# First block's merge: the sum of two gated branches by GpSimd, rounding and remainder of the merged tile one unit later

## The reference, cut to what matters

```python
merged = (jax.nn.sigmoid(g_a) * (y_a @ w_br_a)
          + jax.nn.sigmoid(g_b) * (y_b @ w_br_b)
          + jax.nn.sigmoid(g_c) * (y_c @ w_br_c))
return merged @ w_out
```

## Time and profile before

| what | value |
|---|---|
| median of 3 runs | 3005.26 us (3005.05 to 3005.29) |
| span of the profiled execution | 3003.9 us |
| median of the runs less that span | 1.36 us |
| TensorE busy | 2897.1 us, 96% |
| VectorE busy | 2051.9 us, 68% |
| ScalarE busy | 1366.5 us, 45% |
| GpSimd busy | 153.3 us, 5% |
| merge of layer 0, from its fourth unit to the first product of `out0` | 208.81 to 242.26 us |
| merge of layer 1, likewise | 670.78 to 704.27 us |

### The profile page before, as it was taken

How to read it: one execution, slowest core, us unless ns; L and a number is a source line. 1 busy time by engine, 2 the same in 40 slices (tenths; PEclk the granted TensorE clock), 3 DMA queues, 4 the chain that set the end, 5 groups by cost and what they waited for, 6 DMA issues and landing times.

```text
span 3003.9 us, 59994 instructions
## 1 busy us (share of the span) xinstructions
PE 2897.1 (96%) x23648; PEld 2789.5 (93%) x23648; DVE 2051.9 (68%) x3323; ACT 1366.5 (45%) x2212; POOL 153.3 (5%) x222
## 2 busy tenths in 40 slices
PE   8999999999999999999999999999999999899998
PEld 8889999888999999998889999999999999779998
DVE  4658786658678777778764476867768566876655
ACT  5555445555446432354544354223542235545543
POOL 0000000000000000010000020000200001000000
PEclk9999999999999999999999999999999999999999
DMA  6435764435666565552212354544645445225454
GB/s 235 146 115 187 243 235 163 149 108 176 211 210 198 193 222 194 177 184 67 81 45 89 105 185 161 206 156 171 208 162 207 144 152 187 64 82 192 161 184 138
DMA packets 148053, 487.54 MB, mean 162 GB/s; under 512 B 16400, under 2 KB 25872, under 8 KB 147728
## 3 DMA queue, kind: packets, MB, share of 16 engines
q1 hardware_dynamic: 126688, 407.22, 41.0%
q0 software_dynamic: 21168, 77.60, 7.6%
HBM read 482.66 MB, written 1.05 MB: 161 GB/s over the span
## 4 chain that ended last, share of the span: by engine, by line
PE 82%; DVE 9%; ACT 4%; issue 3%; DMA 2%; POOL 0%; DVEq 0%; ACTq 0%; SPq 0%; POOLq 0%
PE bank L2042 23%; PE bank L2043 22%; PE bank L2044 22%; DVE wlo L1141 3%; ACT whi L606 2%; PE bank L1960 2%; PE bank L1961 2%; PE bank L1962 2%; DVE acc L1742 2%; PE aux L2269 1%; PE bank L2287 1%; DMA bbb<-in_w_ada 1%; PE bank L2120 1%; DMA raw<-in_w_stream 1%; DMA big<-in_w_ada 1%
## 5 line engine op out<-in xcount | busy, mean ns | idle before, releaser
L2042 PE MATMUL bank<-uhi,whi 128*128 128x256 f32 x4968 | 1397.0, 281 | 9.6 <-DVE wlo L1141 6.0
L2044 PE MATMUL bank<-uhi,wlo 128*128 128x256 f32 x4968 | 1381.1, 278 | 0.0
L2043 PE MATMUL bank<-ulo,whi 128*128 128x256 f32 x4968 | 1380.9, 278 | 0.0
L1141 DVE TENSOR_TENSOR wlo<-raw,whi 128x1024 fp32r<-128x1024 f32 (+4 forms) x850 | 951.0, 1121 | 370.7 <-ACT whi L606 362.2
L2042 PEld LDWEIGHTS bank<-uhi,whi 128*128 128x128 f32 x4968 | 935.1, 188 | 28.2 <-issue 22.9
L606 ACT CAST whi<-raw 128x1024 fp32r<-128x1024 f32 (+4 forms) x850 | 811.5, 961 | 282.7 <-PE bank L2044 179.3
L2043 PEld LDWEIGHTS bank<-ulo,whi 128*128 128x128 f32 x4968 | 934.8, 188 | 3.4 <-issue 3.0
L2044 PEld LDWEIGHTS bank<-uhi,wlo 128*128 128x128 f32 x4968 | 937.7, 189 | 0.0
L2042 PE MATMUL bank<-yhi,whi 128*128 128x256 f32 x1740 | 494.1, 284 | 16.2 <-DVE wlo L1141 8.5
L2043 PE MATMUL bank<-ylo,whi 128*128 128x256 f32 x1764 | 491.3, 279 | 0.0
L2044 PE MATMUL bank<-yhi,wlo 128*128 128x256 f32 x1740 | 484.5, 278 | 0.0
(11 more groups left out here) (297 smaller groups left out, 2939.0 us busy)
## 6 DMA issues: line engine op xcount, KB each, us to landing
raw<-in_w_stream SPq DMA_DIRECT2D x674, 512.0 KB, 3.7
big<-in_w_ada POOLq DMA_DIRECT2D x64, 512.0 KB, 3.6
vt<-in_w_ada POOLq DMA_DIRECT2D x51, 512.0 KB, 3.7
raw<-in_w_stream SPq DMA_DIRECT2D x80, 256.0 KB, 2.7
raw<-in_w_stream SPq DMA_DIRECT2D x48, 384.0 KB, 3.1
bbb<-in_w_ada POOLq DMA_DIRECT2D x29, 512.0 KB, 4.7
raw<-in_w_stream SPq DMA_DIRECT2D x32, 192.0 KB, 2.4
raw<-in_w_stream SPq DMA_DIRECT2D x16, 128.0 KB, 2.0
```

The source lines that it names most:

```text
L1141: ve.tensor_tensor(wlo[:, u % SLOTS, 0:n], raw[:, u % SLOTS, 0:n], whi[:, u % SLOTS, 0:n].bitcast(F32), ALU.subtract).then_inc(s_low, 1)
L2042: te.matmul(out_, whi[:, u % SLOTS, w], hi(k)[:, cols], start=k == 0, stop=False)
L2043: te.matmul(out_, whi[:, u % SLOTS, w], lo(k)[:, cols], start=False, stop=False)
L2044: ins = te.matmul(out_, wlo[:, u % SLOTS, w], hi(k)[:, cols], start=False, stop=k == plan.kt[u] - 1)
```

## The change

GpSimd gets a part `merge_pairs(l)`, ahead of its wait for the merge's last unit: for each tile m it waits until the banks of units 3m and 3m + 1 are read (that is, until both gatings are done), adds the two gated branches in place, and gives `s_paired`. VectorE waits for it behind the third gating and makes only the second sum. The rounding of tile m moves on ScalarE from unit 3m + 2 to unit 3m + 3, behind the cast of that unit's `high`, and the remainder on VectorE to the same unit, behind its `low` and gating. For the last tile both stay at unit 23. The gated branches of tiles with even and odd m now lie in different rows of `lg` (0 to 3 and 4 to 7), the merged tile in the fourth of each.

```diff
+MERGE_ROWS = 4
...
+            def merge_pairs(l):
+
+                for m in range(DT):
+                    at = MERGE_ROWS * (m % 2)
+                    pool.wait_ge(*after(U[f"merge{l}"] + 3 * m))
+                    pool.wait_ge(*after(U[f"merge{l}"] + 3 * m + 1))
+                    nc.gpsimd.tensor_tensor(lg[:, at, :], lg[:, at, :], lg[:, at + 1, :], ALU.add).then_inc(s_paired, 1)
+
...
             for name, (first, per, _, _) in plan.ada.items():
+                if name in ("up00", "up10"):
+                    merge_pairs(int(name[2]))
...
-                def evac_m(j, i):
-                    if j % 3 == 2:
-                        val.wait(1)
-                        sc.copy(x1hi[:, 4 * i + j // 3, :], lg[:, 3 + (j // 3) % 2, :]).then_inc(s_ahi, 1)
-                    if j in (4, 7, 10) and isinstance(i, int) and i == 0:
+                def merged(m):
+                    val.wait(1)
+                    sc.copy(x1hi[:, m, :], lg[:, MERGE_ROWS * (m % 2) + 3, :]).then_inc(s_ahi, 1)
+
+                def evac_m(j):
+                    if j % 3 == 0 and j:
+                        merged(j // 3 - 1)
+                    if j in (4, 7, 10):
                         gate_rows(1, (j - 4) // 3)
+                    if j == 23:
+                        merged(DT - 1)
...
-                    ve.tensor_tensor(lg[:, br, :], gates[br][:, m, :], bank(u0, j)[:, 0:S],
+                    ve.tensor_tensor(lg[:, at + br, :], gates[br][:, m, :], bank(u0, j)[:, 0:S],
                                      ALU.mult).then_inc(read(u0, j), 1)
+                    if br == 0 and m:
+                        merged_rest(m - 1)
                     if br == 2:
-                        dve.wait_ge(*after_at(u0, j, i, 12))
-                        mg = lg[:, 3 + (j // 3) % 2, :]
-                        chained(ve.tensor_tensor(lg[:, 0, :], lg[:, 0, :], lg[:, 1, :], ALU.add))
-                        ve.tensor_tensor(mg, lg[:, 0, :], lg[:, 2, :], ALU.add).then_inc(s_val, 1)
+                        dve.wait_ge(*after(u0 + j))
+                        dve.wait_ge(s_paired, DT * l + m + 1)
+                        ve.tensor_tensor(lg[:, at + 3, :], lg[:, at, :], lg[:, at + 2, :], ALU.add).then_inc(s_val, 1)
                         if m == DT - 2:
                             low(u0 + 21 + AHEAD)
-                        ahi.wait(1)
-                        rest(x1lo[:, m, :], mg, x1hi[:, m, :])
+                        if m == DT - 1:
+                            merged_rest(m)
```

More of the change, by code:

```diff
@@ L446, in program @@
         s_hbias = sem("half_bias_ready")
+        s_paired = sem("merge_pair_added")
         ring1 = [bbb[:, 4 * r:4 * r + 4, :] for r in range(2)]
@@ L846, in _ @@
                         high(um + 21 + AHEAD)
-                    evac_m(j % 12, j // 12)
+                    evac_m(j)
                 norm1(f"out{l}", p1("ln1_g", l, DT), p1("ln1_b", l, DT))
@@ L1577, in _, with merged_rest, evac_m @@
                 u0 = U[f"merge{l}"]
[L1579 to L1583, removed]
-                    ve.tensor_tensor(lg[:, br, :], gates[br][:, m, :], bank(u0, j)[:, 0:S],
+                def merged_rest(m):
+                    ahi.wait(1)
+                    rest(x1lo[:, m, :], lg[:, MERGE_ROWS * (m % 2) + 3, :], x1hi[:, m, :])
+                def evac_m(j):
+                    br, m = j % 3, j // 3
+                    at = MERGE_ROWS * (m % 2)
+                    if j % 12 < 3:
+                        dve.wait_ge(s_gate, 6 * l + 3 * (j // 12) + j % 12 + 1)
+                    done(u0, j, 0, 0)
+                    ve.tensor_tensor(lg[:, at + br, :], gates[br][:, m, :], bank(u0, j)[:, 0:S],
                                      ALU.mult).then_inc(read(u0, j), 1)
+                    if br == 0 and m:
+                        merged_rest(m - 1)
                     if br == 2:
-                        dve.wait_ge(*after_at(u0, j, i, 12))
-                        mg = lg[:, 3 + (j // 3) % 2, :]
-                        chained(ve.tensor_tensor(lg[:, 0, :], lg[:, 0, :], lg[:, 1, :], ALU.add))
-                        ve.tensor_tensor(mg, lg[:, 0, :], lg[:, 2, :], ALU.add).then_inc(s_val, 1)
+                        dve.wait_ge(*after(u0 + j))
+                        dve.wait_ge(s_paired, DT * l + m + 1)
+                        ve.tensor_tensor(lg[:, at + 3, :], lg[:, at, :], lg[:, at + 2, :], ALU.add).then_inc(s_val, 1)
                         if m == DT - 2:
                             low(u0 + 21 + AHEAD)
-                        ahi.wait(1)
-                        rest(x1lo[:, m, :], mg, x1hi[:, m, :])
+                        if m == DT - 1:
+                            merged_rest(m)
                 for j in range(24):
```

## The result

The changed kernel takes 2992.39 us (median of five runs, 2984.0 to 2998.1). Beside it the kernel before had a median of 3005.29 (five runs, 3005.05 to 3022.96). The ratio is 0.9938 with a 95% interval of 0.9909 to 0.9967.

The account below looks back on a forecast made before the run. VectorE with its turn to ScalarE bounds the merges, 4.80 us a tile against TensorE's 4.10. Gains of 4.2 (layer 1) and 3.9 (layer 0) sum to 8.1, giving 2997.2 us; own range 2995.5 to 2999.2, with rivals 2993.3 to 3002.0.

Parts of the forecast that it names:

- The bound and the loop: In the merges VectorE with its turn to ScalarE bounds, 4.80 us a tile; forecast 4.4 in sigmoid tiles, 4.0 otherwise.
- (a): First sum of each merged tile leaves VectorE: 0.46 us less per tile.
- (b): Rounding and remainder move later: the 0.47 us wait is covered, and 0.52 until the next `wlo` becomes 0.34.
- (c): VectorE waits for GpSimd's sum ahead of its last one; the sum takes 0.73 us and excludes `wlo`, not gatings.
- The stops: TensorE's seven waits per layer for a tile's first `wlo`, 0.44 us in the tile read; forecast down to one or two.
- Late stop: TensorE's wait in the output projection for the last merged tile's remainder: 1.14 us in layer 1, forecast 1.1 to 1.4.
- The 0.3 taken off for slower products in layer 0: Layer 0's gain set at 4.2 - 0.3 = 3.9 us, its products being taken as slower there.
- 0.1 to 0.2 for transfers that are closer together: At the merge's end, a cost of 0.1 to 0.2 us set against a 0.3 to 0.4 gain.
- GpSimd costs more: Rival, chance 0.26: loop 4.4 to 4.6 us throughout, 5 us gained in all, 3000.2 us.
- gives nothing: Rival, chance 0.04: the pair-sum wait replaces the rounding's and the late DMA chain decides, 3005.3 us.
- starves: Rival, chance 0.05: GpSimd sums of 2.7 us make the loop 5.35 us, 3.3 us slower per layer, 3011.9 us.
- TensorE alone is the bound: Rival, chance 0.20: the merges' stops vanish, 9.5 to 11.9 us gained, middle 10.5, time 2994.8 us.

Follow-up runs that it names:

- (a) alone: Changed kernel with rounding and remainder put back at unit 3m + 2, GpSimd's sum kept: mean 3002.00 us over 12 runs.
- (b) alone: Changed kernel with both sums on VectorE, rounding and remainder in the new order: mean 2996.85 us over 12 runs.
- the later sigmoids: Changed kernel with the three late sigmoids one unit later on ScalarE, behind a tile's third cast: mean 2988.46 us over 30 runs.
- the doubled sum: Changed kernel with a second, unused GpSimd sum ahead of each pair sum: mean 3005.38 us over 12 runs.
- the earlier cast: Changed kernel with late sigmoids one unit later and the merge's fourth weight cast ahead of its first three sigmoids: mean 2991.68 us over 19 runs.
- the two further edits: On top of later sigmoids: fourth weight's cast ahead of the first sigmoids (2991.68 us), then also the seventh tile's rounding at unit 21 (2988.30 us).

## Why the prediction was right, and where it failed

**The bound and the loop** were right: VectorE's turn with ScalarE, 4.80 us against 4.10. Under 4.10 TensorE sets the pace; the last sums of layer 1 start at 671.66, 676.09, 680.52, 684.95, 688.88, 692.81 and 696.75, steps of 4.43 three times and 3.93 three times, for 4.4 and 4.0 forecast.

**(a) and (b).** "The 0.47 wait is covered": it is gone in the changed profile and back in the old order. The new order was the larger part, 7.1 of 8.3 us. The prediction priced the parts in VectorE's loop (0.46, 0.47, 0.18) but not in the end time; together they bring the loop under TensorE's 4.10, and from there the next part earns nothing. (a) alone gave 2.1 us, (b) alone 7.1, both 8.3. The 0.46 of (a) alone came to 0.1 a tile, because of the 0.37 wait for GpSimd.

**(c) GpSimd's sum.** 0.74 where alone, 1.06 behind `wlo`, where 1.2 to 1.4 was forecast for a blocked one. The forecast let the sum's whole 0.73 follow `wlo`; the runs show that such a sum ends 0.58 to 0.61 after it, whether the `wlo` takes 0.69 or 1.22, as the earlier trace rows already had it (1767.66 - 1767.07 = 0.59). That is 0.1 of the 4.0, the loop being 3.93 (only the sum behind the output projection's 128x1024 `wlo` took that and more, 1.59 at 701.63). `wlo` behind GpSimd took 1.17. The gatings took their 0.41 beside it. That the sigmoid decides who is first is shown by the later sigmoids.

**The stops.** One or two forecast behind the first, some 0.3 to 0.4 us in all; measured two slivers, 0.11 us with 0.2 for their slow first products, so 0.3.

**The end of the merge.** Late stop forecast at 1.1 to 1.4 and about as before, measured 0.83, 4.13 for 4.2 us gained in layer 1 and 3.56 for 3.9 in layer 0. The stop is not shorter because the remainder came sooner: the stop ends 35.5 us after the stretch's start, as forecast (706.25 - 670.78), but TensorE came to it after 34.7 us for the 34.0 forecast, since the 42 products ahead took 5.2 us (a small stop at 701.21 among them) and not 4.8. That this error left the sum alone is luck: the remainder decides the end. The 0.3 taken off for slower products in layer 0 fits that one execution, in which its stretch has 109 slow steps for 15 in layer 1; the other two profiles before have 52 for 77 and 76 for 74, so it isn't a trait of the layer. Of the "0.1 to 0.2 for transfers that are closer together" I made no measurement by itself.

**The sum** of the merges, 8.1 us, is 7.7 in the pair of first profiles and 8.3 over seven. The rivals that GpSimd costs more, gives nothing or starves are out: the first wanted a loop of 4.4 to 4.6 in every tile, and half of them take 3.93; none of the 16 sums in the first profile of the changed kernel took more than 1.59 us, where starving wanted 2.2. *TensorE alone is the bound* is what the later sigmoids made of the kernel, at 10.1 us for the 10.5 that it was priced at.

**The step that failed** is the last: "The profiled execution spans 3003.9 us, which would become 2995.8; the runs (median 3005.26) lie 1.4 above the span, so 2997.2", and with it "No change and 0.2% (6.0 us, about what a measurement of this kernel can tell)" and an own range of 2995.5 to 2999.2. The step takes three runs 0.24 us apart for the kernel's level, lets everything outside the merges come out the same, and gives all width of the range to the mechanism and none to the measurement. The runs showed a standard deviation of 7.4 us over 152 runs of the kernel before (2987.19 to 3022.96); the mean of five such runs is uncertain by 3.3 us (7.4 / √5), and the range was missed by 0.9. The mechanism held and the sum of the merges was right to 0.2 to 0.4 us. The miss of 4.8 us parts so: 1.3 because the level is 3003.95 and not 3005.26; 0.2 from the merges (8.3 for 8.1); 2.7 by which the changed kernel's mean gain, 11.0, is above the merges'; 0.55 because the five runs' median is under the mean of all 42, 2992.94. The 2.7 has a bound of ±2.7 and is hardly told apart from nothing; its cause stays open. That the direction came out was earned, for the merges' gain alone gives it; of the 4.8 us by which it missed, 1.9 are the chance of few runs and 2.7 stay open.

**What stays open** is the surplus of the later sigmoids, 15.5 ±2.6 for 10.1. That a faster merge makes later code faster is not borne out by the other kernels: those with both sums on VectorE gave 7.1 for 7.1 and 8.8 for 9.5, the doubled sum -1.4 for 0.6, the earlier cast, which holds the same edit, 12.3 for 11. Nor do the counts of slow steps tell it: 6774, 6471 and 6114 with later sigmoids, 4191 and 5209 with the earlier cast. I know no cause. What makes TensorE's pace the one or the other was not found either.

The fastest versions measured are those with the sigmoids one unit later, alone or with the two further edits: pooled 2988.3 to 2991.7 us. The bounds don't part them from each other.

## What to carry to other kernels

Where an engine is late by a hand-over to another and back, moving the answer one unit later can give more than taking work off it; here about 7.1 of 8.3 us. Put the parts' savings on the loop, not on the end: once it is under the pace of the engine that bounds, the rest earns nothing, and an instruction that only decides who goes first can matter as much as the next offload (here the sigmoids' place gave 1.8 us, GpSimd's sum 1.2). And read a stage's own gain from its stretch in the trace; the whole time of this kernel needed 42 runs against 152 for a bound of 2.7 us. Even the stretch needs more than one profile, and a look at TensorE's pace in it.

## What the runs showed of the hardware

- TensorE makes the same products, always busy and at a granted clock of 1.00, at either of two paces: 56.7 or 58.9 us for 500. Pieces of 24 to 2500 products run at the one or the other, some in the same place in each execution, many not. It spreads the runs more than this change moves them.
- GpSimd and VectorE take turns at instructions with all operands in the on-chip memory. A 128x256 sum on GpSimd takes 0.74 us alone, 1.06 begun 0.23 into a 0.69 `wlo`, 1.18 when a `wlo` held back by the sum ahead runs first, 1.59 begun 0.23 into a 1.22 one. A sum begun within a `wlo` ends 0.58 to 0.61 after it in each of these cases, less than its 0.74. The blocked VectorE instruction ended 0.29 to 0.56 after GpSimd's. The Trainium skill says so in "SBUF — State Buffer", section "Who interferes with whom": the later one is fully blocked; the 1.17 for 0.69 agrees.
- GpSimd's sum gave 1.2 us with the new order and 2.1 without, each by one profile of the kernel that leaves one part out, and cost nearly all that the change gave when it was made twice. The Trainium skill, "GPSIMD Engine Reference", section "4.1 Engine selection", advises VectorE for such a sum, GpSimd being about twice as slow on two inputs. The duration agrees (0.74 for 0.42); a loss from a single sum is seen in no run here.
